# Head projections of a latent attention layer: key tiles first, values in 512 column blocks, exponentials in groups of three

## The chip, the cores and the metric

One core of one Trainium2 chip runs the whole program. Its engines are TensorE (PE; weight loads are shown as PEld), VectorE (DVE), ScalarE (ACT), GpSimd (POOL) and SyncE (SP), which issues the weight transfers. The metric is the device time of one execution in microseconds (us). The times of the kernel before are 4355.25, 4356.09 and 4361.63 us, median 4356.09.

## What is computed

The program is a first block of two layers, then a second block of two layers, an even one and an odd one. The change touches the odd one alone, and in it what stands between the latents and the attention:

```python
cq, ckv, kr = split(h @ w_in, (384, 640))              # 512 latents of x, 256 of the context (768 for keys and values)
q  = (rms_norm(cq, qa_norm) @ w_uq).reshape(n, 16, 64 + 32)
kv = (rms_norm(ckv, kva_norm) @ w_ukv).reshape(n, 16, 64 + 64)
q_nope = rms_norm(q[..., :64], qn_nope);  q_rope = rope_2d(rms_norm(q[..., 64:], qn_rope))
k_nope = rms_norm(kv[..., :64], kn_nope); v = kv[..., 64:]
k_rope = rope_2d(rms_norm(kr[:, :, None, :], kn_rope)) # one for all heads
# rms_norm(x, g) = x * rsqrt(mean(x * x) + eps) * g
y = softmax([q_nope, q_rope] @ [k_nope, k_rope] * scale) @ v @ w_out
```

## The kernel before

Each product in high precision is three TensorE products (`mm3`, L193 to L198): both factors are split into a high and a low part, and high with high, high with low and low with high are summed in PSUM. Weights come in tiles of 128 x 1024 floats (512 KB) through the `Stream` (L121): SyncE loads three slots ahead, `split_hi` on ScalarE (L167) copies the high part, `split_lo` on VectorE (L174) takes the low part as the rest. There are two slots of split tiles, so tile n+2 can be split once tile n is used (`used`). SyncE loads again after `lo_done`.

The odd layer (L1765) has 16 heads and works in two halves of 8 heads. In each half `HeadTiles` (L790) makes queries Q, keys K and values V, then `Attention` (L521) runs 32 units on them. Attention of a half begins on TensorE (L588) when all of the half's heads are out (`all_out`), and heads of the second half begin on TensorE when the first attention is done. So the stages stand one behind the other.

`HeadTiles` runs over a list of items. The first half begins with the rotary key `kr_tile` (8 x 3 products of 512 and 8 x 3 of 256 columns on the layer's input). Then for each pair of heads, four pairs a half: two `q_tile` items (9 products of 512 columns each), one `k_tile` (6 of 512 and 6 of 256), one `v_tile`: 36 products of 128 columns, with the latents as stationary and 128 weight columns as moving factor. A pair has two weight tiles of its own, each partly filled: 16 tiles for both halves. For each item but a value item:

- TensorE projects into two PSUM banks, chosen by the item's number; ScalarE squares them (L855) and copies them raw (L859).
- TensorE sums the squares over the rows of a head with a matrix of ones (L827, plain fp32) into banks 4 and 5.
- ScalarE takes the logarithm (`Ln`, L866) and then exp(-0.5 x) of it (`Exp`, L873) at once: the inverse root. The compiler puts an ACT_TABLE_LOAD before each of the two, and the profile shows it under the same line.
- VectorE multiplies raw, gain and inverse root: for queries and kr into a temporary (L890), for keys straight into K (L895).
- For queries and kr, TensorE turns the result with the rotation matrix (L835), VectorE multiplies it by the cosine (L905) and the sine (L907) and adds (L912); for kr the sum goes to eight heads of K, each add followed by a copy (L914).

TensorE's program takes, for item i: project i, sum the squares of i-1, turn i-2. ScalarE: square and copy i, then Ln and Exp of i-1. The raw copy and the temporary have two buffers, the root and its inverse one each. A value item is one ScalarE copy of 768 columns into V (L851). `split_hi` stands before the square.

Of the kernel before, what the change touches and what calls it, by code (L numbers as in the profile page):

```python
# [27 lines left out]
KC = D // 128  # L28
# [21 lines left out]
ODD_TILES = 6 + 2 * ODD_PAIRS + 8  # L50
# [3 lines left out]
def program(nc, io):  # L54
# [11 lines left out]
    with top:  # L66
# [858 lines left out]

        def setup():
# [838 lines left out]
        def odd_layer(CX):  # L1765
# [3 lines left out]
            with ExitStack() as ctx:  # L1769
                Hh, Hl = sb(ctx, "h_hi", [128, KC, T], F32R), sb(ctx, "h_lo", [128, KC, T], F32R)  # L1770
                Ch, Cl = sb(ctx, "c_hi", [128, KC, CT], F32R), sb(ctx, "c_lo", [128, KC, CT], F32R)
# [14 lines left out]
                def carve(at, shape):  # L1786
# [45 lines left out]
                def q_tile(n, h):  # L1832
                    def go(pe, i, done):
                        st.ready(pe, n)
                        for k in range(3):
                            m = mm3(pe, ps[:, 2 * (i % 2), :], st.at(n, 256 * k + 128 * h, 256 * k + 128 * h + 128),
                                    (Qh[:, k, :], Ql[:, k, :]), k == 0, k == 2)
                        m.then_inc(done, 1)
                    return go

                def k_tile(n):
                    def go(pe, i, done):
                        st.ready(pe, n)
                        for s, (a, e) in enumerate(((0, T), (T, N2))):
                            for k in range(2):
                                m = mm3(pe, ps[:, 2 * (i % 2) + s, 0:e - a], st.at(n, 256 * k, 256 * k + 128),
                                        (Lh[:, k, a:e], Ll[:, k, a:e]), k == 0, k == 1)
# [3 lines left out]
                def v_tile(n):  # L1851
# [11 lines left out]
                for half in range(2):  # L1863
                    items = []
                    if half == 0:
# [308 lines left out]
```

## Time and profile before

| what | us |
|---|---|
| median of three runs | 4356.09 |
| the profiled execution, its own time | 4354.72 |
| its span | 4353.2 |
| TensorE busy | 3941.1 (91%) |
| VectorE busy | 2270.2 (52%) |
| ScalarE busy | 1586.7 (36%) |

The span is what the profile shows from first to last instruction; the time has 1.5 us more around it. The page's groups of instructions name a line, an engine, what is written from what, their count, their busy time, the mean of one, and the idle time before them with what ended it. Averages over the span mix all layers. The odd layer's heads and attentions take 330 us of it, about 7.6%, and have to be read from windows of their own. The granted clock is a share of TensorE's full 2.4 GHz: 0.5 is its lower level, 1.2 GHz.

### The profile page before, as it was taken

What the parts mean: (1) busy time and instruction counts of PE and PEld (TensorE: products, weight loads), DVE (VectorE), ACT (ScalarE), POOL (GpSimd) and SP (SyncE); (2) the same over time, 40 slices, a digit from 0 to 9 for tenths busy, and PEclk for the clock granted to TensorE, in tenths of its full rate; (3) what the DMA queues carried; (4) which work ended last, traced back from release to release, by engine and by line L of the source; (5) the groups of instructions that cost most, each with busy time, mean ns of one, the idle gap of its engine ahead of it and who ended that gap; (6) DMA issues with size and microseconds to landing.
All of it is one profiled execution on the core that took longest, in us unless ns stands there. A gap on an engine that the chain in (4) does not pass through costs nothing. (4 is left out here: it accounts for less than half of the span.)

```text
span 4353.2 us, 52924 instructions
## 1 busy us (share of the span) xinstructions
PE 3941.1 (91%) x19258; PEld 3213.4 (74%) x19258; DVE 2270.2 (52%) x4044; ACT 1586.7 (36%) x2672; POOL 126.5 (3%) x188
## 2 busy tenths in 40 slices
PE   5999978999899997999969999699998679798999
PEld 3887766888688776688848887588887457576887
DVE  3665563666566666366632454355555344444555
ACT  2223353222322336322255454322221574743222
POOL 1000000000100000000000000000000000000000
PEclk9999989999999998999989999899999889899999
DMA  6443202443544220244211110121221110102332
GB/s 239 135 136 100 63 25 78 136 130 111 186 131 140 82 73 15 87 136 144 88 57 53 44 42 24 48 63 59 62 63 49 30 39 1 39 1 73 97 96 77
DMA packets 99854, 354.04 MB, mean 81 GB/s; under 512 B 11139, under 2 KB 14723, under 8 KB 98776
## 3 DMA queue, kind: packets, MB, share of 16 engines
q1 hardware_dynamic: 76632, 274.64, 20.8%
q0 software_dynamic: 18304, 70.33, 5.0%
q10 hardware_dynamic: 4736, 6.62, 0.4%
q8 instruction: 117, 1.92, 0.2%
q14 instruction: 65, 0.53, 0.0%
HBM read 345.73 MB, written 11.06 MB: 82 GB/s over the span
## 5 line engine op out<-in xcount | busy, mean ns | idle before, releaser
L167 ACT ACTIVATE w_hi<-w_raw 128x1024 fp32r<-128x1024 f32 x500 | 529.4, 1060 | 1902.5 <-PE ps L198 1733.9
L174 DVE TENSOR_TENSOR w_lo<-w_raw,w_hi 128x1024 fp32r<-128x1024 f32 x500 | 615.0, 1231 | 1161.2 <-ACT w_hi L167 1160.8
L196 PE MATMUL ps<-h_hi,w_hi 128*128 128x512 f32 (+1 forms) x2824 | 1094.2, 387 | 66.6 <-DVE h_lo L255 34.2
L197 PE MATMUL ps<-h_lo,w_hi 128*128 128x512 f32 (+1 forms) x2824 | 1083.3, 384 | 0.0
L198 PE MATMUL ps<-h_hi,w_lo 128*128 128x512 f32 (+1 forms) x2824 | 1082.1, 383 | 0.0
L196 PEld LDWEIGHTS ps<-h_hi,w_hi 128*128 128x128 f32 x2824 | 537.2, 190 | 192.3 <-issue 54.9
L198 PEld LDWEIGHTS ps<-h_hi,w_lo 128*128 128x128 f32 x2824 | 537.8, 190 | 103.9
L197 PEld LDWEIGHTS ps<-h_lo,w_hi 128*128 128x128 f32 x2824 | 538.8, 191 | 100.4 <-issue 1.4
L196 PE MATMUL ps<-a_hi,w_hi 128*128 128x512 f32 x1472 | 549.0, 373 | 3.3 <-DVE ctx_x L454 3.3
L197 PE MATMUL ps<-a_lo,w_hi 128*128 128x512 f32 x1472 | 546.8, 371 | 0.0
L198 PE MATMUL ps<-a_hi,w_lo 128*128 128x512 f32 x1472 | 546.0, 371 | 0.0
L196 PEld LDWEIGHTS ps<-a_hi,w_hi 128*128 128x128 f32 x1472 | 277.0, 188 | 57.2 <-DVE ctx_x L454 6.3
L198 PEld LDWEIGHTS ps<-a_hi,w_lo 128*128 128x128 f32 x1472 | 276.8, 188 | 49.1
L197 PEld LDWEIGHTS ps<-a_lo,w_hi 128*128 128x128 f32 x1472 | 277.1, 188 | 47.6
L454 DVE SCALAR_TENSOR_TENSOR x<-ps,x 128x512 f32<-128x512 f32 x352 | 231.5, 685 | 54.6 <-PE ps L198 52.6
L454 DVE SCALAR_TENSOR_TENSOR x<-ps,mod,x 128x512 f32<-128x512 f32 x256 | 188.0, 748 | 94.0 <-PE ps L198 94.0
L402 ACT ACTIVATE a_hi<-val 128x512 fp32r<-128x512 f32 (+1 forms) x184 | 106.0, 592 | 307.2 <-DVE val L438 307.2
L662 ACT ACTIVATE arena<-arena,nm 128x768 f32<-128x768 f32 (+3 forms) x160 | 130.9, 818 | 218.0 <-DVE nm L720 217.4
L240 PE MATMUL ps<-scratch,ones 128*128 128x512 f32 (+1 forms) x144 | 76.2, 682 | 98.8 <-ACT scratch L220 98.8
L612 PE MATMUL ps<-ident,arena 128*128 128x128 f32 x784 | 119.2, 284 | 31.7 <-DVE h_lo L775 26.4
L419 DVE TENSOR_TENSOR a_lo<-val,a_hi 128x512 fp32r<-128x512 f32 (+1 forms) x184 | 115.2, 640 | 62.5 <-ACT a_hi L402 62.5
L240 PEld LDWEIGHTS ps<-scratch,ones 128*128 128x128 f32 x144 | 27.3, 223 | 144.8 <-ACT scratch L220 124.2
(243 smaller groups left out, 4661.9 us busy)
## 6 DMA issues: line engine op xcount, KB each, us to landing
w_raw<-in_w_first SPq DMA_DIRECT2D x316, 512.0 KB, 3.6
w_raw<-in_w_mlp SPq DMA_DIRECT2D x128, 512.0 KB, 3.6
shared<-in_w_ada POOLq DMA_DIRECT2D x96, 512.0 KB, 4.3
w_raw<-in_w_odd SPq DMA_DIRECT2D x30, 512.0 KB, 3.6
w_raw<-in_w_even SPq DMA_DIRECT2D x26, 512.0 KB, 3.6
near_stage<-near_bias POOLq DMA_DIRECT2D x32, 256.0 KB, 2.9
bias_rows<-bias_line SPq DMA_DIRECT2D x1, 5120.0 KB
shared<-silu_cond POOLq DMA_DIRECT2D x4, 1024.0 KB, 4.9
```

The source lines that it names most:

```text
L167: act.activation(self.hi[:, n % H, :], self.raw[:, n % R, :], ACT.Copy).then_inc(self.hi_done, 1)
L174: dve.tensor_tensor(self.lo[:, n % self.n_hl, :], self.raw[:, n % self.n_raw, :], self.hi[:, n % self.n_hl, :].bitcast(F32), ALU.subtract) ...
L196: pe.matmul(out, lhs[0], rhs[0], start=start, stop=False)
L197: pe.matmul(out, lhs[0], rhs[1], start=False, stop=False)
L198: return pe.matmul(out, lhs[1], rhs[0], start=False, stop=stop)
L240: pe.matmul(self.acc(), ones[:, :], self.tmp["sq"][:, c % 2, 0:self.n], start=(c == 0), stop=(c == self.nk - 1)).then_inc(self.sum_done, 1)
L402: m = act.activation(self.hi[s][:, 2 * (c % 2) + j, :], self.val[s][:, j, :], ACT.Copy)
L419: m = dve.tensor_tensor(self.lo[s][:, a, :], self.val[s][:, j, :], self.hi[s][:, a, :].bitcast(F32), ALU.subtract)
L454: m = dve.scalar_tensor_tensor(out=stream["x"][:, o, :], in0=ps[:, self.down_bank(8 * c + o, s), 0:stream["n"]], scalar=self.gains(s, o), ...
L612: m = pe.transpose(ps[:, 4 + t % 2, 128 * j:128 * j + 128], tmp["s"][:, u % 2, 128 * (b + j):128 * (b + j) + 128], ident[:, :])
L662: act.activation(tmp["s"][:, u % 2, 0:n], tmp["s"][:, u % 2, 0:n], ACT.Exp, bias=tmp["nm"][:, u % 16:u % 16 + 1], scale=-1.0, accum_out=tm ...
```

## The change

Both halves now have five full weight tiles: one with the keys of all eight heads, three with the queries, one with the values. That makes 24 tiles in the layer's stream in place of 30. `HeadGroups` takes the place of `HeadTiles` in the odd layer (the even layer keeps the old class):

- Items: kr (first half only), four key items, eight query items. That is 13 items in the first half and 12 in the second. Values are no items: they are six blocks of 128 latents x 512 weight columns (6 products each), projected behind the last item, two before the last item's sums and four behind. Each is copied to V with one ScalarE copy of 512 columns.
- Exponentials: items are taken in groups of three. Ln of each item comes as before, one item behind the square; Exp of a whole group comes right behind the Ln of its last item. So roots have six buffers, raw copies five. Exp writes over the root, the scaling writes over the raw copy.
- VectorE: once a group's Exp are there, it scales all items of the group, then turns those that have a rotary part. On TensorE, item k's rotation stands g[-1] + 2 + (k - g[0]) iterations into the program, for a group g: two to four items behind where it stood.
- The fifth raw buffer: from item 5 on, the raw copy waits until the item five back is out (`item_out`).
- `split_hi` now stands behind the raw copy.
- The raw copies lie where the context's split input lay, the squares where the raw copies lay.

The core of the diff (indentation shortened):

```diff
-ODD_TILES = 6 + 2 * ODD_PAIRS + 8
+ODD_TILES = 6 + 2 * 5 + 8
...
+class HeadGroups:
+    RAW, ROOT = 5, 6
+    BLOCKS = 6
...
+        self.groups = [range(a, min(a + group, L)) for a in range(0, L, group)]
+        self.ends = {g[-1]: g for g in self.groups}
+        self.parts = [sum(not x["frees"] for x in items[:k]) for k in range(L + 1)]
+        self.ropes = [sum(x["rope"] for x in items[:k]) for k in range(L + 1)]
+        self.turn_after, at = {}, 0
+        for g in self.groups:
+            for k in g:
+                if items[k]["rope"]:
+                    at = max(at, g[-1] + 2 + k - g[0])
+                    self.turn_after.setdefault(at, []).append(k)
...
+    def value_bank(self, j):
+        return (2 * (len(self.items) % 2) + j) % 4
+    def tensor(self, pe):
+        items, w, L = self.items, self.w, len(self.items)
+        def sums(k):
+            pe.wait_ge(self.sq_done, k + 1)
+            if k:
+                pe.wait_ge(self.root_done, k)
+            for a, b in self.halves(items[k]["n"]):
+                m = pe.matmul(ps[:, 4 + a // 512, 0:b - a], items[k]["ones"], w["sq"][k % 2][:, a:b],
+                              start=True, stop=True)
+            m.then_inc(self.sum_done, 1)
+        def turn(k):
+            r = self.ropes[k]
+            pe.wait_ge(self.t_done, k + 1)
+            if r >= 2:
+                pe.wait_ge(self.sin_done, r - 1)
+            pe.matmul(ps[:, 6 + r % 2, 0:512], self.rot, w["raw"][k % self.RAW][:, 0:512],
+                      start=True, stop=True).then_inc(self.rotated, 1)
+        def value_block(j):
+            if j in (0, 2):
+                pe.wait_ge(self.raw_done, L - 1 + j // 2)
+            if j >= 4:
+                pe.wait_ge(self.v_out, j - 3)
+            return self.values["project"](pe, j, self.value_bank(j))
+        for i in range(max(L + 1, max(self.turn_after, default=0) + 1)):
+            if i < L:
+                if i >= 2:
+                    pe.wait_ge(self.raw_done, i - 1)
+                items[i]["project"](pe, i, self.st.used if items[i]["frees"] else self.projected)
+            if 1 <= i <= L:
+                if i == L:
+                    value_block(0).then_inc(self.v_mm, 1)
+                    value_block(1).then_inc(self.v_mm, 1)
+                sums(i - 1)
+                if i == L:
+                    for j in range(2, self.BLOCKS):
+                        value_block(j).then_inc(self.v_mm if j < self.BLOCKS - 1 else self.st.used, 1)
+            for k in self.turn_after.get(i, ()):
+                turn(k)
+    def scalar(self, act):
+        items, w, L = self.items, self.w, len(self.items)
+        def inverse_root(k):
+            act.wait_ge(self.root_done, k + 1)
+            root = w["root"][k % self.ROOT][:, 0:items[k]["n"]]
+            act.activation(root, root, ACT.Exp, scale=-0.5).then_inc(self.inv_done, 1)
+        for i in range(L + 1):
+            if i < L:
+                it = items[i]
+                if it["frees"]:
+                    act.wait_ge(self.st.used, it["frees"][-1] + 1)
+                else:
+                    act.wait_ge(self.projected, self.parts[i] + 1)
+                if i >= 2:
+                    act.wait_ge(self.sum_done, i - 1)
+                act.activation(w["sq"][i % 2][:, 0:it["n"]], self.pair(i, 0, it["n"]), ACT.Square
+                               ).then_inc(self.sq_done, 1)
+                if i >= self.RAW:
+                    self.item_out(act, i - self.RAW)
+                act.activation(w["raw"][i % self.RAW][:, 0:it["n"]], self.pair(i, 0, it["n"]), ACT.Copy
+                               ).then_inc(self.raw_done, 1)
+                for n in it["tiles"]:
+                    self.st.split_hi(act, n + self.st.n_hl)
+            if i >= 1:
+                k, n = i - 1, items[i - 1]["n"]
+                act.wait_ge(self.sum_done, k + 1)
+                if k >= self.ROOT:
+                    act.wait_ge(self.t_done, k - self.ROOT + 1)
+                act.activation(w["root"][k % self.ROOT][:, 0:n],
+                               ps[:, 4:6, :].rearrange("p a n -> p (a n)")[:, 0:n], ACT.Ln,
+                               bias=eps[:, 0:1], scale=items[k]["scale"]).then_inc(self.root_done, 1)
+                for e in self.ends.get(k, ()):
+                    inverse_root(e)
+        for j in range(self.BLOCKS):
+            if j < self.BLOCKS - 1:
+                act.wait_ge(self.v_mm, j + 1)
+            else:
+                act.wait_ge(self.st.used, self.values["tile"] + 1)
+            act.activation(self.values["dst"](j), ps[:, self.value_bank(j), :], ACT.Copy).then_inc(self.v_out, 1)
+        self.st.split_hi(act, self.values["tile"] + self.st.n_hl)
+    def vector(self, dve):
+        items, w, L = self.items, self.w, len(self.items)
+        def scale(k):
+            it, n = items[k], items[k]["n"]
+            raw, inv = w["raw"][k % self.RAW], w["root"][k % self.ROOT]
+            dve.wait_ge(self.inv_done, k + 1)
+            if it["rope"]:
+                dve.scalar_tensor_tensor(out=raw[:, 0:n], in0=raw[:, 0:n], scalar=it["gain"], in1=inv[:, 0:n],
+                                         op0=ALU.mult, op1=ALU.mult).then_inc(self.t_done, 1)
+                return
+            for r, dst in it["dst"]:
+                m = dve.scalar_tensor_tensor(out=dst(0, n), in0=raw[r, 0:n], scalar=it["gain"][r, :],
+                                             in1=inv[r, 0:n], op0=ALU.mult, op1=ALU.mult)
+            m.then_inc(self.t_done, 1)
+        def turn(k):
+            it, r, raw = items[k], self.ropes[k], w["raw"][k % self.RAW]
+            if it["rope"]:
+                if r:
+                    dve.wait_ge(self.out_done, r)
+                dve.wait_ge(self.t_done, k + 1)
+                dve.tensor_tensor(w["cos"], raw[:, 0:512], self.cos, ALU.mult).then_inc(self.cos_done, 1)
+                dve.wait_ge(self.rotated, r + 1)
+                dve.tensor_tensor(w["sin"], ps[:, 6 + r % 2, 0:512], self.sin, ALU.mult).then_inc(self.sin_done, 1)
+                dve.wait_ge(self.cos_done, r + 1)
+                dve.wait_ge(self.sin_done, r + 1)
+                for rows, dst in it["dst"]:
+                    m = dve.tensor_tensor(dst(0, 512), w["cos"][rows, :], w["sin"][rows, :], ALU.add)
+                    if it["n"] > 512:
+                        m = dve.tensor_copy(dst(512, it["n"]), raw[rows, 512:it["n"]])
+                m.then_inc(self.out_done, 1)
+        for i in range(L):
+            for n in items[i]["tiles"]:
+                self.st.split_lo(dve, n + self.st.n_hl)
+            for g in self.groups:
+                if g[-1] + 1 == i:
+                    for k in g:
+                        scale(k)
+                    for k in g:
+                        turn(k)
+        for k in self.groups[-1]:
+            scale(k)
+        for k in self.groups[-1]:
+            turn(k)
+        self.st.split_lo(dve, self.values["tile"] + self.st.n_hl)
+    def all_out(self, eng):
+        eng.wait_ge(self.v_out, self.BLOCKS)
+        eng.wait_ge(self.t_done, len(self.items))
+        eng.wait_ge(self.out_done, self.ropes[-1])
+    def item_out(self, eng, k):
+        if self.items[k]["rope"]:
+            eng.wait_ge(self.out_done, self.ropes[k] + 1)
+        else:
+            eng.wait_ge(self.t_done, k + 1)
...
-        Ch, Cl = sb(ctx, "c_hi", [128, KC, CT], F32R), sb(ctx, "c_lo", [128, KC, CT], F32R)
+        with ExitStack() as early:
+            Ch, Cl = sb(early, "c_hi", [128, KC, CT], F32R), sb(early, "c_lo", [128, KC, CT], F32R)
+        raw_slots = sb(ctx, "head_raw", [128, 2 * KC * CT])
...
-        w = {"raw": cx[:, 0:2 * N2].rearrange("p (a n) -> p a n", a=2), "sin": cx[:, 2 * N2:2 * N2 + 512],
-             "sq": carve(0, [2, N2]), "root": carve(2 * N2, [N2]), "inv": carve(3 * N2, [N2]),
-             "t": carve(4 * N2, [2, N2]), "cos": carve(6 * N2, [512])}
+        w = {"raw": [raw_slots[:, N2 * k:N2 * k + N2] for k in range(5)],
+             "root": [carve(N2 * k, [N2]) for k in range(6)],
+             "sq": [cx[:, N2 * k:N2 * k + N2] for k in range(2)],
+             "cos": carve(6 * N2, [512]), "sin": cx[:, 2 * N2:2 * N2 + 512]}
...
-                for j in range(6):
-                    t = slice(128 * j, 128 * j + 128)
-                    for k in range(2):
-                        m = mm3(pe, ps[:, 2 * (i % 2) + j // 4, 128 * (j % 4):128 * (j % 4) + 128],
-                                (Lh[:, k, t], Ll[:, k, t]), st.at(n, 256 * k + 128, 256 * k + 256), k == 0, k == 1)
...
+        def q_tile(n, h):
             def go(pe, i, done):
-                for j in range(6):
-                    t = slice(128 * j, 128 * j + 128)
-                    for k in range(2):
-                        m = mm3(pe, ps[:, 2 * (i % 2) + j // 4, 128 * (j % 4):128 * (j % 4) + 128],
-                                (Lh[:, k, t], Ll[:, k, t]), st.at(n, 256 * k + 128, 256 * k + 256), k == 0, k == 1)
+                for k in range(3):
+                    tile, c = n + (3 * h + k) // 8, 128 * ((3 * h + k) % 8)
+                    st.ready(pe, tile)
+                    m = mm3(pe, ps[:, 2 * (i % 2), :], st.at(tile, c, c + 128), (Qh[:, k, :], Ql[:, k, :]),
+                            k == 0, k == 2)
+                    if c == 896 and k < 2:
+                        m.then_inc(st.used, 1)
                 m.then_inc(done, 1)
+            return go
+        def v_block(n):
+            def go(pe, j, bank):
+                st.ready(pe, n)
+                t = slice(128 * j, 128 * j + 128)
+                for k in range(2):
+                    m = mm3(pe, ps[:, bank, :], (Lh[:, k, t], Ll[:, k, t]), st.at(n, 512 * k, 512 * k + 512),
+                            k == 0, k == 1)
+                return m
             return go
...
+            for h in range(8):
+                ends = {2: first + 1, 5: first + 2, 7: first + 3}
+                items.append({"project": q_tile(first + 1, h), "n": T, "ones": mla_ones[:, :],
+                              "scale": 1.0, "gain": gq[:, 0:1], "rope": True,
+                              "tiles": [ends[h]] if h in ends else [], "frees": [first + 3] if h == 7 else [],
+                              "dst": [(slice(0, 96), lambda a, b, c=h: Q[0:96, c, a:b])]})
+            values = {"project": v_block(first + 4), "tile": first + 4, "dst": lambda j: V[:, j, :]}
+            heads.append(HeadGroups(S, w, st, items, 3, values, rot[:, :], cos[:, :], sin[:, :]))
...
+    for half in range(2):
+h = slice(8 * half, 8 * half + 8)
+keys = ukv[:, :, h, 0].reshape(2, 128, 4, 128).transpose(1, 2, 0, 3).reshape(1, 128, 1024)
+queries = uq[:, :, h].transpose(1, 2, 0, 3).reshape(128, 3, 1024).transpose(1, 0, 2)
+values = ukv[:, :, h, 1].transpose(1, 0, 2, 3).reshape(1, 128, 1024)
+odd += [keys, queries, values]
```

## Rows read from the trace of the kernel before

**Rows 1.** Windows view: stretch, length, busy us (count) by engine, granted clock, DMA.

```profile
3463.42:3578.31 114.89, 90.71 (x366) 66.72 (x367) 48.95 (x68) 80.26 (x91) 0.00 (x0) 0.83 0.14 42
3578.31:3700.87 122.56, 111.92 (x721) 91.19 (x721) 58.12 (x184) 51.55 (x112) 0.00 (x0) 0.96 0.00 1
3700.87:3793.66 92.79, 72.20 (x313) 52.55 (x313) 38.97 (x48) 73.28 (x84) 0.00 (x0) 0.87 0.16 46
```

**Rows 2.** Groups of ScalarE, 3463 to 3794 us: busy, mean ns | idle.

```profile
L866 ACT ACT_TABLE_LOAD x25 | 32.1, 1283 | 0.4
L873 ACT ACT_TABLE_LOAD x25 | 32.1, 1283 | 0.4
...
L866 ACT ACTIVATE arena<-ps,eps 128x512 f32<-128x512 f32 (+1 forms) x25 | 19.1, 764 | 0.3
L689 ACT ACTIVATE arena<-ps 128x512 f32<-128x512 f32 x32 | 18.5, 578 | 6.9 <-PE ps L612 6.9
L167 ACT ACTIVATE w_hi<-w_raw 128x1024 fp32r<-128x1024 f32 x17 | 18.0, 1057 | 37.1 <-PE ps L198 37.1
L873 ACT ACTIVATE arena<-arena 128x512 f32<-128x512 f32 (+1 forms) x25 | 17.7, 707 | 0.3
L859 ACT ACTIVATE ctx_x<-ps 128x512 f32<-128x512 f32 (+1 forms) x25 | 16.8, 670 | 1.0
...
L851 ACT ACTIVATE v<-ps 128x768 f32<-128x768 f32 x8 | 6.3, 792 | 0.0
```

**Rows 3.** Timeline, a query tile's chain: start, length, instruction, idle before.

```profile
3508.30 1.28 ACT L866 ACT_TABLE_LOAD   x1
...
3509.59 0.69 ACT L866 ACTIVATE arena<-ps,eps 128x512 f32<-128x512 f32 x1
...
3510.43 1.10 PE L827 MATMUL ps<-arena,mla_ones 128*128 128x512 f32 x2 [1.32 <-ACT arena L866]
3511.59 0.63 ACT L873 ACTIVATE arena<-arena 128x512 f32<-128x512 f32 x1
...
3512.26 0.75 DVE L890 SCALAR_TENSOR_TENSOR arena<-ctx_x,q_gain,arena 128x512 f32<-128x512 f32 x1 [3.69 <-ACT arena L873]
```

**Rows 4.** Timeline of TensorE: neighbouring products, 128 and 512 columns.

```profile
3492.75 0.28 PE L198 MATMUL ps<-w_hi,ckv_lo 128*128 128x128 f32 x1
...
3492.86 0.28 PE L196 MATMUL ps<-w_hi,ckv_hi 128*128 128x128 f32 x1
...
3529.55 0.39 PE L196 MATMUL ps<-cq_hi,w_hi 128*128 128x512 f32 x1
...
3529.78 0.39 PE L197 MATMUL ps<-cq_lo,w_hi 128*128 128x512 f32 x1
```

**Rows 5.** The windows view, four stretches of 5 us, columns as in rows 1.

```profile
3465.00:3470.00 5.00, 5.00 (x15) 3.90 (x14) 0.00 (x0) 0.00 (x0) 0.00 (x0) 0.58 0.00 0
3490.00:3495.00 5.00, 4.36 (x34) 3.91 (x34) 4.90 (x12) 4.02 (x5) 0.00 (x0) 1.00 0.00 0
3515.00:3520.00 5.00, 5.00 (x25) 5.00 (x25) 2.07 (x4) 2.75 (x4) 0.00 (x0) 0.50 0.00 0
3700.00:3705.00 5.00, 4.13 (x11) 3.30 (x12) 0.77 (x4) 0.33 (x1) 0.00 (x0) 0.66 0.00 0
```

**Rows 6.** The timeline, the end of the second heads stretch.

```profile
3782.93 1.50 PE L827 MATMUL ps<-arena,head_ones 128*128 128x512 f32 x4
...
3784.27 1.02 PE L835 MATMUL ps<-arena,rot 128*128 128x512 f32 x2
...
3793.66 1.19 PE L588 MATMUL ps<-k,q 128*128 128x512 f32 x1 [8.36 <-DVE q L912]
```

**Rows 7.** The groups of VectorE over 3463 to 3794 us.

```profile
L890 DVE SCALAR_TENSOR_TENSOR arena<-ctx_x,q_gain,arena 128x512 f32<-128x512 f32 x16 | 12.0, 752 | 56.7 <-ACT arena L873 56.6
...
L907 DVE TENSOR_TENSOR ctx_x<-ps,sin 128x512 f32<-128x512 f32 x17 | 11.6, 684 | 0.0
...
L912 DVE TENSOR_TENSOR k<-arena,ctx_x 32x512 f32<-32x512 f32 x8 | 5.4, 677 | 0.1
```

More of the change, by code:

```diff
@@ L923, in all_out, with __init__, pair, halves @@
                     eng.wait_ge(self.out_done, self.ropes[-1])
+        class HeadGroups:
+            RAW, ROOT = 5, 6
+            BLOCKS = 6
+            def __init__(self, S, work, st, items, group, values, rot, cos, sin):
+                self.items, self.st, self.w, self.values = items, st, work, values
+                self.rot, self.cos, self.sin = rot, cos, sin
+                self.projected, self.sq_done, self.raw_done, self.sum_done = S("proj"), S("hsq"), S("raw"), S("hsum")
+                self.root_done, self.inv_done, self.t_done = S("hroot"), S("hinv"), S("ht")
+                self.rotated, self.cos_done, self.sin_done, self.out_done = S("rot"), S("cos"), S("sin"), S("hout")
+                self.v_mm, self.v_out = S("v_mm"), S("v_out")
+                L = len(items)
+                self.groups = [range(a, min(a + group, L)) for a in range(0, L, group)]
[8 more added lines that the diff above has]
+                            self.turn_after.setdefault(at, []).append(k)
+            def pair(self, i, a, b):
+                return ps[:, 2 * (i % 2):2 * (i % 2) + 2, :].rearrange("p a n -> p (a n)")[:, a:b]
+            @staticmethod
+            def halves(n):
+                return [(0, min(n, 512))] + ([(512, n)] if n > 512 else [])
+            def value_bank(self, j):
[131 more added lines that the diff above has]
+                    eng.wait_ge(self.t_done, k + 1)
@@ L1830, in kr_tile, with k_tile @@
                     project_x(pe, 5, 2 * (i % 2), xs).then_inc(done, 1)
[L1832 to L1841, printed above, removed]
+                def k_tile(n, p):
                     def go(pe, i, done):
@@ L1864, in odd_layer @@
                     items = []
+                    first = 6 + 5 * half
                     if half == 0:
-                        items.append({"project": kr_tile, "n": N2, "plain": False, "ones": mla_ones[:, :], "scale": 1.0,
-                                      "gain": vec("kr_norm", 1), "rope": True, "tiles": [5],
+                        items.append({"project": kr_tile, "n": N2, "ones": mla_ones[:, :], "scale": 1.0,
+                                      "gain": vec("kr_norm", 1), "rope": True, "tiles": [5], "frees": [5],
@@ L1868, in odd_layer @@
                                       "dst": [(kr_rows, lambda a, b, h=h: K[64:96, h, a:b]) for h in range(8)]})
                     for p in range(4):
-                        n = 6 + 2 * (4 * half + p)
-                        for h in range(2):
-                            items.append({"project": q_tile(n, h), "n": T, "plain": False, "ones": mla_ones[:, :],
-                                          "scale": 1.0, "gain": gq[:, 0:1], "rope": True, "tiles": [] if h == 0 else [n],
-                                          "dst": [(slice(0, 96), lambda a, b, c=2 * p + h: Q[0:96, c, a:b])]})
@@ L1875, in odd_layer @@
-                        items.append({"project": k_tile(n + 1), "n": N2, "plain": False, "ones": head_ones[:, :],
-                                      "scale": 1.0 / HD, "gain": vec("kn_norm", 1), "rope": False, "tiles": [],
+                        items.append({"project": k_tile(first, p), "n": N2, "ones": head_ones[:, :],
+                                      "scale": 1.0 / HD, "gain": vec("kn_norm", 1), "rope": False,
+                                      "tiles": [first] if p == 3 else [], "frees": [first] if p == 3 else [],
@@ L1884, in odd_layer @@
-                    heads.append(HeadTiles(S, w, st, items, rot[:, :], cos[:, :], sin[:, :]))
+                    for h in range(8):
[4 more added lines that the diff above has]
+                                      "dst": [(slice(0, 96), lambda a, b, c=h: Q[0:96, c, a:b])]})
```

15 lines of the change are left out of this document (3 added, 12 removed).

## The prediction

> **What bounds the kernel now.** I read the page's share of busy time first, and it misleads here: TensorE at 91% is a mean over all layers, and the change touches only the odd layer's heads. So I cut windows at the places where one stage hands over to the next: the first product of the rotary key, the first product of each attention, and the first product of the second half's heads [rows 1]. The reader is to see two head stretches, of 114.89 and 92.79 us (207.68 together), in which ScalarE is busy 80.26 and 73.28 us (70% and 79%), TensorE 90.71 and 72.20 us with a granted clock of 0.83 and 0.87, and VectorE under half. The attention between them has a clock of 0.96 and isn't touched. Since attention begins only when the last head is out, whatever a head stretch loses or gains counts fully.
>
> Next come ScalarE's groups over the same time [rows 2]. Of its 153.5 us in the two head stretches, 64.2 us are table loads: 25 under the logarithm's line and 25 under the exponential's, 1.283 us each, one ahead of every such instruction. The chain of one query tile shows what they do [rows 3]: load 1.28, logarithm 0.69, load 1.28, exponential 0.63, and only then does VectorE go on, after 3.69 us idle; TensorE stood 1.32 us for the logarithm. With a single root buffer and two of everything else, nobody gets ahead of this chain. So the stretch is bound by ScalarE's list, and TensorE waits in pieces of 1 to 3 us.
>
> The third view is TensorE's pace. Neighbours of 128 columns stand 0.11 us apart and neighbours of 512 columns 0.23 us [rows 4]: four times the columns for twice the time. The clock comes last [rows 5]: of the two windows full of a value item's 128 column products one shows 1.00 and one 0.50 for the whole 5 us. In the second TensorE had stood with gaps before, fell to its 1.2 GHz level, and stayed there as long as the 128 column products ran; three of the eight value items look like this. The windows at the start of each half show 0.58 and 0.66.
>
> **A yardstick.** To put a price on a rearranged order I wrote the three engines' lists out in program order and gave each instruction the duration of its row; each starts when its engine is free and the event it waits for is there, with 0.05 us for a hand-over (an exponential ends at 3512.22, VectorE starts at 3512.26) and 0.2 us for TensorE after a real wait (the logarithm ends at 3510.28, the sums begin at 3510.43) [rows 3]. The sums of squares take TensorE 0.86 us for 512 columns and 1.3 for 768 (3782.93 to 3784.27 [rows 6]), which is also the source of 0.86 for a rotation. Run on the order of before, at the full clock, this gives 96.6 and 81.7 us. The mean clocks 0.83 and 0.87 say that 34% and 26% of the stretches, 39 and 24 us, were at the lower level. Some 3 us of each lie in the idle end, and half of the rest is lost: 18 and 10.5 us. Together 114.6 and 92.2, against 114.89 and 92.79. The method carries.
>
> **What the change does, part by part.**
>
> *Table loads.* Groups of three give one load ahead of the group's logarithms and one ahead of its exponentials: 5 groups in the first half, 4 in the second, so 18 loads in place of 50. 32 x 1.283 = 41.1 us leave ScalarE [rows 2]. The trace shows the next instruction 1.29 us after a load starts and nothing besides, so 1.28 is the whole price. The Trainium skill (ScalarE: Activation LUTs, What ACT_TABLE_LOAD costs) puts a switch at about 2.66 us, a drain included; by that the 32 would be 85 us, but no row here has the drain. The same page (Table sets: the hidden batching unit) says that logarithm and exponential can share a set, by which there would be no load to save; the 25 and 25 loads of rows 2 say that this program doesn't use it.
>
> *Values.* 8 x 36 products at 0.11 us are 32 us at the full clock; 2 x 36 products at 0.23 us are 16.4 us [rows 4]. 15 us leave TensorE, and more at the lower level. ScalarE copies 12 x 0.58 us in place of 8 x 0.79 [rows 2], a wash.
>
> *Weight tiles.* Six fewer: 6.3 us off ScalarE [rows 2], 7.4 off VectorE, six transfers off SyncE's queue, which was waiting for slots and not for data. Worth nothing by itself beyond ScalarE's list.
>
> *New waits.* By list sums TensorE would have 62.4 and 51.9 us, ScalarE 53 and 47, VectorE 43 and 33. The bound moves to TensorE and to what makes it wait. At each group's edge ScalarE does load, three exponentials, square, copy, load and logarithm, about 6.5 us, while TensorE has two projections (4.1) and then waits for the root: 2.5 to 3.3 us once per group. In the first half, item 5's raw copy waits for the rotary key's output, whose eight adds (0.68 [rows 7]) and eight copies keep VectorE 6.5 us: ScalarE stands 6.3 us, with squares and logarithms queued behind that copy, and TensorE 4.8. Later a query tile's low part is queued behind item 5's turn on VectorE: TensorE stands 2.3 us. Each `q_tile` now checks its weight tile before each third: 16 more checks a half that nearly always find the tile there. [...]
>
> *The tail.* It gets longer. Before, the second half ended with 9.4 us from TensorE's last rotation to attention's first product, 8.36 of them idle [rows 6]. Now value blocks 4 and 5 wait for banks, that is for ScalarE's copies, which stand behind the last exponentials; the rotation of item 8 stands behind block 5; and on VectorE its sine and add, a 1.2 us low part, three scalings (0.75) and three turns (0.69 + 0.68 + 0.69 each [rows 7]) stand behind that rotation. From the last exponential that is 15.2 us.
>
> **The new order written out, at the full clock.** Second half: third key's exponential at 18.5 us, then the three query groups at 30.6, 43.2 and 55.3 (12.3 us each: 8.7 of products and sums, up to 2.6 of rotations, the edge's wait), end at 70.5. First half: 8.3 us for the rotary key, first group out at 24.1, then 41.9 (17.8: the stand for the rotary key's output), 53.6, 68.8 (15.2: three rotations and the late tile), 74.0 for the single last item, end at 87.4.
>
> **The sum.** Lower level at the start, as now [rows 5]: 2.9 and 1.7 us. Further stretches at the lower level cannot be read from before; between none and the 15 and 9 us of before I take two short ones a half, 3.4 us lost in each half, since gaps stay but no 128 column products prolong them. Hand-overs a little longer than 0.05: 1 us a half, since doubling them adds 1.4 and 0.7 to the new order. First half 87.4 + 2.9 + 3.4 + 1.0 = 94.7; second 70.5 + 1.7 + 3.4 + 1.0 = 76.6; with 1 us for the checks 172.3. Saved: 207.7 - 172.3 = 35.4 us. The profiled execution had a time of 4354.72, so 4319.3; the median of the runs is 1.4 us above it: 4320.7 us. Nothing ahead of the heads changes but where buffers lie; attention starts, as before, after an idle TensorE; the output projection's first two tiles are split ahead of attention, as before.
>
> **Rivals.** *The queues couple more tightly than my order says*, so that every group costs what the dearest ordinary one does, 15.2 us in place of about 12. For it: raw copy, rotation and low part wait across three queues. Against: the yardstick hit both halves of before within 0.6 us. Six groups x 3 us = 18 us less saved: 4338.
>
> *TensorE never waits inside a half.* Lists of 62.4 and 51.9 plus tails of 13 and 15 and the 4.6 at the start are 147 us: 61 us saved, 4295. Against: the key output's stand is in the program, whatever the durations.
>
> *The other side: the clock.* Gaps of 2 to 5 us at every group edge drop TensorE to 1.2 GHz, and it stays there. With all of both halves at that level my order gives 128.4 and 104.8 = 233.2 us, 25.5 more than now: 4381.6. Between that and 157.9 without any, it turns slower when TensorE is at the lower level for two thirds of the stretch. For it: before had 34% and 26%. Against: the long low stretches were those of the 128 column products, which are gone; 512 column products brought 1.00 back within the kernel's own first tile.
>
> *The change doesn't do what it says*: the compiler puts loads ahead of every exponential all the same. Nothing between three neighbouring exponentials asks for another table; I give it next to nothing, inside the first rival.
>
> **How the numbers follow.** My order 0.72 (its own range 4309 to 4331), tighter coupling 0.16, no waits 0.06, the clock 0.03, none of them 0.03. Range for 8 in 10: 4306 to 4338. A measurement of this kernel can tell 0.2%, 8.7 us, from no change; for that 26.7 of the 35.4 us would have to be lost, which only the far end of the coupling case or a middling case of the clock does: faster 0.94, same 0.04, slower 0.02.
>
> **What the profile after would show.** 18 loads; no 128 column products in the heads; ScalarE about 53 and 47 us busy in the stretches, TensorE at a clock of 0.85 to 0.95; the stretches 92 to 98 and 74 to 80 us long; a 6 us stand of ScalarE at a raw copy early in the first half; the tails 13 to 15 us from the last exponential. The prediction is wrong if the stretches are right but attention or later layers move by more than 3 us, if the clock is below 0.75, or if VectorE's turns stand in the way of more than one raw copy.

## The result and the profile after

Five executions of the changed kernel took 4322.10, 4330.21, 4331.93, 4334.69 and 4335.02 us, median 4331.93, against 4356.09 before: ratio 0.9942, 95% interval 0.993 to 0.9955, so 24 us or 0.6% faster. In a second group of runs the same kernel had a median of 4326.08 (ratio 0.9927, 0.9907 to 0.9947). The forecast was 4320.7, range 4306 to 4338.

The profiled execution is the fastest of the five, 4322.10 us with a span of 4320.5. Its windows, cut at the same events as [rows 1] (first heads, first attention, second heads; the columns are those of [rows 1]):

```profile
3462.05:3556.92 94.87, 74.89 (x258) 50.30 (x259) 44.46 (x65) 55.03 (x74) 0.00 (x0) 0.88 0.09 28
3556.92:3684.93 128.01, 117.32 (x720) 94.93 (x721) 59.10 (x185) 51.67 (x112) 0.00 (x0) 0.91 0.02 5
3684.93:3761.93 77.00, 60.84 (x204) 39.68 (x205) 34.49 (x45) 48.39 (x67) 0.00 (x0) 0.90 0.09 28
```

The heads take 94.87 and 77.00 us in place of 114.89 and 92.79, 35.8 us less, with ScalarE down from 80.26 and 73.28 us busy to 55.03 and 48.39. But the first attention, whose code is the same, takes 128.01 us in place of 122.56, at a clock of 0.91 in place of 0.96.

ScalarE's groups from 3462.05 to 3761.93 us, both head stretches and the attention between them (columns of [rows 2]; L1034 is the logarithm, L1010 the exponential, L1025 the raw copy, L1021 the square):

```profile
L1034 ACT ACTIVATE arena<-ps,eps 128x512 f32<-128x512 f32 (+1 forms) x25 | 19.1, 765 | 10.1 <-PE ps L969 10.0
L1025 ACT ACTIVATE head_raw<-ps 128x512 f32<-128x512 f32 (+1 forms) x25 | 16.8, 671 | 6.5 <-DVE k L1077 6.5
L1021 ACT ACTIVATE ctx_x<-ps 128x512 f32<-128x512 f32 (+1 forms) x25 | 16.7, 667 | 30.8 <-PE ps L198 30.8
...
L1034 ACT ACT_TABLE_LOAD x9 | 11.5, 1283 | 0.2
L1010 ACT ACT_TABLE_LOAD x9 | 11.5, 1283 | 0.2
```

50 loads have become 18. Where the logarithm used to wait for nothing (0.3 us before, the groups of [rows 2]: ScalarE was always late), it now waits 10.0 us for TensorE's sums, the square 30.8 us for projections, and the raw copy 6.5 us for VectorE. ScalarE's list no longer sets the length of the stretch.

The timeline of the first half at the stand behind the rotary key, and of the second half's end (columns of [rows 3]; L978 is the rotation, L1071 the sine, L1055 a scaling):

```profile
3500.39 0.60 ACT L1025 ACTIVATE head_raw<-ps 128x512 f32<-128x512 f32 x1 [6.55 <-DVE k L1077]
```

```profile
3744.48 1.67 ACT L1010 ACTIVATE arena<-arena 128x512 f32<-128x512 f32 x3
3746.06 2.04 ACT L1044 ACTIVATE v<-ps 128x512 f32<-128x512 f32 x4
...
3749.56 1.02 PE L978 MATMUL ps<-head_raw,rot 128*128 128x512 f32 x2
...
3750.61 0.69 DVE L1071 TENSOR_TENSOR ctx_x<-ps,sin 128x512 f32<-128x512 f32 x1 [9.20 <-PE ps L978]
...
3752.02 1.22 DVE L174 TENSOR_TENSOR w_lo<-w_raw,w_hi 128x1024 fp32r<-128x1024 f32 x1
3753.16 2.07 DVE L1055 SCALAR_TENSOR_TENSOR head_raw<-head_raw,q_gain,arena 128x512 f32<-128x512 f32 x3
...
3761.93 1.19 PE L588 MATMUL ps<-k,q 128*128 128x512 f32 x1 [3.60 <-DVE q L1075]
```

Here stand three of the places where the gain is given back. ScalarE stands 6.55 us at a raw copy until the rotary key is out. The last exponential ends at 3746.15 and attention starts at 3761.93, a tail of 15.8 us. In it VectorE idles 9.20 us for one rotation that is queued on TensorE behind the value blocks, which wait for ScalarE's value copies. Before, this tail was 4.35 us, because the last exponential belonged to a key item, which has no rotation:

```profile
3788.47 0.84 ACT L873 ACTIVATE arena<-arena 128x768 f32<-128x768 f32 x1
```

### The profile page after: what moved, and what is told of

Read it like the earlier page. It is cut to its first block and busy times, and to the rows that moved or that the text cites. A ratio compares the mean times of both kernels' runs of the same rounds, so it can differ in the third digit from the quotient of the medians.

```text
span 4320.5 us, 52368 instructions
## 1 busy us (share of the span) xinstructions
PE 3914.2 (91%) x19042; PEld 3185.2 (74%) x19042; DVE 2263.0 (52%) x4038; ACT 1536.5 (36%) x2638; POOL 125.4 (3%) x188
## 5 line engine op out<-in xcount | busy, mean ns | idle before, releaser
L198 PEld LDWEIGHTS ps<-a_hi,w_lo 128*128 128x128 f32 x1472 | 276.9, 188 | 48.8
```

The source lines that it names most:

```text
L198: return pe.matmul(out, lhs[1], rhs[0], start=False, stop=stop)
```

## Experiments

All times of head stretches are from one trace each; "heads" is the sum of both. The kernel before was traced three times, its heads are 207.7, 202.1 and 210.6 us (mean 206.8); the changed kernel twice, 171.9 and 171.7 (mean 171.8). Each variant has one trace, two_turn_early a second one (best_again). The old kernel's traces spread over 8.5 us, so a smaller difference that rests on single traces is weak evidence by itself.

**The same kernels again.** 

> The changed kernel once more, unaltered. Theory: the two head stretches repeat within 1 us (94.9 and 77.0), and what differs between executions is TensorE's granted clock in the other stages, so that the span follows the mean clock: 0.955 went with 4320.5, 0.951 with 4333. Rival: the head stretches themselves vary by several us.

> The kernel before, unaltered, for a second trace of it. Question: the forecast took 207.7 us for its two head stretches from one execution. Theory (what the clock does in the other stages made the median gain smaller than the forecast): the head stretches repeat within 2 us, and the part ahead of them lies anywhere between 3462 and 3473 us, as in the eight traces of kernels that don't differ there. Rival (the one execution was a slow one in the heads): 203 us or less.

> The same kernel, a third trace of it, with the same expectations as for the second.

The windows of both head stretches: the changed kernel's second trace, then the second and third trace of the kernel before.

```profile
3470.58:3564.78 94.20, 72.86 (x258) 48.62 (x259) 44.44 (x65) 55.03 (x74) 0.00 (x0) 0.90 0.09 28
3688.29:3765.75 77.46, 61.46 (x205) 40.26 (x205) 34.48 (x45) 48.37 (x67) 0.00 (x0) 0.90 0.09 28
```

```profile
3462.60:3571.91 109.31, 88.45 (x366) 65.01 (x367) 48.93 (x68) 79.83 (x91) 0.00 (x0) 0.84 0.15 44
3694.56:3787.32 92.76, 72.20 (x312) 52.62 (x313) 38.95 (x48) 73.28 (x84) 0.00 (x0) 0.87 0.16 46
```

```profile
3466.23:3581.18 114.95, 90.78 (x366) 66.73 (x367) 48.94 (x68) 80.30 (x91) 0.00 (x0) 0.83 0.14 42
3703.74:3799.34 95.60, 77.13 (x312) 56.12 (x313) 38.96 (x48) 73.31 (x84) 0.00 (x0) 0.82 0.15 45
```

The changed heads repeat within 0.7 us. The old ones spread over 8.5 us, where 2 were expected: before_once (4348.45 us in all) has 202.1, under the 203 that the rival named, and before_twice (4357.83 us) has 210.6. The forecast's base of 207.7 lies within 1 us of the mean of the three. So it was fair, but in part by luck: before_once would have moved the forecast saving by 5.6 us. What differs between executions is the rest: the first head stretch begins at 3462.05 in one trace of the changed kernel and at 3470.58 in the other, and nothing ahead of it differs. The run times follow the mean clock: of the changed kernel's nine executions the three at 0.951 took 4329.4 to 4335.0 us, the two at 0.955 and 0.956 took 4322.1 and 4319.3.

**Loads put back.**

```diff
-heads.append(HeadGroups(S, w, st, items, 3, values, ...))
+heads.append(HeadGroups(S, w, st, items, 1, values, ...))
```

> Group size 1 in place of 3: each exponential behind its own logarithm again, 50 loads in place of 18, all else of the change kept. Theory (the queues' order sets the stretch, and with five raw buffers most of a load lies beside TensorE's work): the hand schedule gives 87.8 and 75.8 us in place of 87.4 and 70.5 at the full clock, so the two head stretches together grow by 6 us, to about 178. Rival (the loads removed are what the change gained): 32 x 1.283 = 41 us, to about 213.

```profile
3462.50:3556.19 93.69, 73.41 (x258) 48.16 (x259) 45.51 (x65) 76.47 (x90) 0.00 (x0) 0.92 0.10 28
3682.00:3764.06 82.06, 60.68 (x204) 38.90 (x205) 35.37 (x45) 69.92 (x83) 0.00 (x0) 0.92 0.08 26
```

ScalarE is 43 us busier (76.47 and 69.92 against 55.03 and 48.39), all of it the 32 loads and what comes with them, and the heads take 175.8 us, 3.9 more; the first half is even shorter. The median was 4324.86, no different from the changed kernel's 4326.08 in the same runs. So the exponentials in groups of three, as this kernel makes them, are worth about 4 us in one trace and nothing that the total can show. The rival's 41 us falls. Read the other way: with all 50 loads in place the rest of the change already takes 31 of the 35 us off the old heads.

**Groups of two.** The same edit with 2.

> Group size 2 in place of 3: 26 loads in place of 18. Theory: shorter groups free TensorE and VectorE earlier and shorten the tail by one turn; the schedule gives 78.2 and 68.1 in place of 87.4 and 70.5, so 11.6 us less in the head stretches although 8 loads (10.3 us of ScalarE) come back. Rival (each load is paid): 10 us more.

```profile
3462.93:3546.37 83.44, 69.34 (x259) 47.27 (x259) 44.49 (x65) 60.49 (x78) 0.00 (x0) 0.93 0.11 32
3671.17:3743.44 72.27, 59.42 (x205) 39.08 (x205) 34.43 (x45) 53.62 (x71) 0.00 (x0) 0.90 0.10 30
```

Heads 155.7 us, 16 less than in threes, with 8 loads more; median 4306.68, ratio to before 0.9892 (0.9873 to 0.9911). The Trainium skill (ScalarE: Activation LUTs, Rules for kernel authors) says to group by table set and to do all of one set before switching. Here that holds only up to the point where the group makes others wait: from one to two it gains 20 us in the heads, from two to three it loses 16. Two of these waits can be read off. ScalarE's stand at the raw copy is 6.5 us in threes, and 0.0 in twos and in ones. The two tails, from the last exponential to attention, are 14.6 and 15.8 us in threes, 12.5 and 13.6 in twos, 9.5 and 10.1 in ones.

**Loads taken away, old order and new.** In the heads' traces table loads stand ahead of logarithms and exponentials only, none ahead of a copy.

```diff
-act.activation(..., ACT.Exp, scale=-0.5)      # the inverse roots of the odd layer's heads
+act.activation(..., ACT.Copy, scale=-0.5)
```

> The kernel before, with the odd layer's exponentials of the roots replaced by scaled copies, so that nothing switches the table between logarithms: some 48 of 50 loads fall away (heads get the wrong scale; that part of the computation is changed). Theory: in the old order, with two buffers, loads lie on the path. The hand schedule gives 81.3 and 68.0 us at the full clock in place of 96.6 and 81.7, 29 us less, and up to 10 more where the clock rises. Rival (loads lie beside TensorE's work in the old order too, as one_per_group showed for the new one): under 6 us less.

> The changed kernel with the same replacement: 16 of its 18 loads fall away (heads get the wrong scale). Theory: the schedule gives 81.4 and 62.9 in place of 87.4 and 70.5, 13.6 us less: the two loads at each group's edge are still on the path, although spreading them out (one_per_group) cost next to nothing. Rival (loads are all hidden now): under 3 us less.

The kernel before without loads, then the changed kernel without loads:

```profile
3465.75:3551.92 86.17, 76.24 (x366) 56.16 (x367) 48.95 (x68) 48.28 (x67) 0.00 (x0) 0.96 0.19 55
3677.47:3748.84 71.37, 63.35 (x312) 46.98 (x313) 39.15 (x48) 44.43 (x62) 0.00 (x0) 0.96 0.21 60
```

```profile
3471.76:3559.51 87.75, 69.51 (x259) 47.36 (x259) 44.45 (x65) 44.30 (x66) 0.00 (x0) 0.91 0.09 30
3683.06:3749.24 66.18, 58.12 (x204) 38.29 (x205) 34.30 (x45) 40.05 (x61) 0.00 (x0) 0.94 0.11 32
```

Four loads are left in the two stretches of either kernel, in each half one ahead of the first logarithm and one ahead of attention's first exponential, which found its table loaded before. So 46 loads fall away from the old order and 14 from the new one, and not 48 and 16 as the expectations had it.

In the old order the loads were worth 49 us: heads 157.5 in place of 206.8 for 46 loads, 59 us of ScalarE. The medians say the same: 4307.23 in place of 4355.63, 48.4 us. 29 were expected from the order at the full clock and up to 10 from the clock, which rose from 0.83 and 0.87 to 0.96 although the 128 column products were all still there; both terms were too small together by 10. In the changed kernel the last 14 are worth 18 us (153.9 in place of 171.8), as much as they take on ScalarE, 18.0 us (13.6 expected). Without loads old and new order differ by 3.6 us in one trace each, and not at all in the medians (4307.23 and 4308.96). So what the whole rewrite gains depends on the loads: it is a way to live with them. Once they are gone, fewer tiles and wide value products are offset by the new order's own waits.

**Narrow value products in the new order.**

```diff
-m = mm3(pe, ps[:, bank, :], latents, st.at(n, 512 * k, 512 * k + 512), ...)
+for c in range(0, 512, 128):      # four products of 128 columns for each of 512
+    m = mm3(pe, ps[:, bank, c:c + 128], latents, st.at(n, 512 * k + c, 512 * k + c + 128), ...)
```

> Each value block as four times 128 weight columns in place of one 512 column product (144 products a half in place of 36), all else kept. Theory: 24 x 0.11 = 2.7 us a block in place of 1.4; the schedule gives 94.6 and 76.6 in place of 87.4 and 70.5, 13 us more in the two head stretches, and up to 7 us more where the clock falls and stays low under these products. Rival (value products lie beside ScalarE's chain anyway): under 3 us more.

```profile
3464.39:3579.92 115.53, 94.88 (x367) 71.33 (x367) 44.44 (x65) 55.24 (x74) 0.00 (x0) 0.78 0.07 23
3703.38:3786.49 83.11, 68.70 (x312) 48.90 (x313) 34.46 (x45) 48.48 (x67) 0.00 (x0) 0.91 0.08 26
```

Heads 198.6 us, 26.8 more; median 4349.55 of ten executions, 23.5 us over the changed kernel's in the same runs, ratio to before 0.9988. In this order most of the gain is gone without the wide products. The second half grew by 6.1 us, as the schedule had it, with the same 128 column products at a clock of 1.00. The first grew by 20.7: TensorE had waited 2.80 us for the value tile's low part, began the blocks at 3537.42, fell to its lower level within 3 us and stayed there to their end. Six neighbouring windows of 5 us, 3540 to 3570, read 0.50 with TensorE busy all the time; the first of them:

```profile
3540.00:3545.00 5.00, 5.00 (x25) 5.00 (x25) 1.00 (x2) 0.00 (x0) 0.00 (x0) 0.50 0.37 129
```

**Two raw buffers and 50 loads.**

```diff
-RAW, ROOT = 5, 6
+RAW, ROOT = 2, 6          # and groups of one, as in one_per_group
```

> As one_per_group, but with two raw buffers in place of five. Theory (in the new order with 50 loads it is the raw buffers that keep ScalarE going past VectorE's turns): item i's raw copy now waits for the output of item i - 2; the schedule gives 121.9 and 100.8 us at the full clock in place of 87.8 and 75.8, 59 us more, to about 235 for both. Rival (the order of items and the value blocks carry it, buffers don't matter): under 10 us more.

```profile
3467.99:3599.98 131.99, 83.86 (x259) 52.93 (x259) 45.80 (x65) 77.55 (x90) 0.00 (x0) 0.84 0.07 20
3722.51:3832.05 109.54, 70.01 (x205) 42.66 (x205) 35.65 (x45) 70.90 (x83) 0.00 (x0) 0.86 0.07 20
```

```profile
PE ps L969 <- ACT arena L1034: 31.9, 12, 8.4
DVE head_raw L1055 <- ACT arena L1010: 31.0, 8, 4.6
ACT head_raw L1025 <- DVE q L1075: 22.0, 6, 4.0
```

Heads 241.5 us, 65.8 more than with five buffers (59 expected), and 4390 us for the single execution: slower than before. The waits of the first half (who waits for whom, us in total, times, longest) show the ring: ScalarE's raw copy waits for VectorE's output, VectorE for the exponential, TensorE for the logarithm. So the five buffers are what makes 50 loads harmless in one_per_group.

**A rotation moved ahead.** Groups of two, and in each half the rotation that stood behind the last value blocks:

```diff
 if i == L:
-    for j in range(2, self.BLOCKS): value_block(j)...
-for k in self.turn_after.get(i, ()): turn(k)
+    for j in (2, 3): value_block(j)...
+    for k in self.turn_after.get(i, ()): turn(k)
+    for j in (4, 5): value_block(j)...
+# for i != L the rotations stay where they were
```

> Groups of two, and the rotation that stood behind value blocks 4 and 5 moved ahead of them (behind block 3). Theory: VectorE's sine, add, low part, scalings and last turns start before ScalarE's value copies are through; the schedule gives 76.2 and 64.1 in place of 78.2 and 68.1 of two_per_group, 6 us less in the head stretches, about 4301 us. Rival (the tail is set by the value copies): within 2 us of two_per_group.

> two_turn_early once more, with more rounds. Theory: head stretches of 148 us in both, 24 us under the changed kernel, 59 under the kernel before; the median between 4296 and 4309 us. Rival (its gain over two_per_group in the stretches is not kept): median at or above 4307.

```profile
3471.19:3552.13 80.94, 69.20 (x258) 47.29 (x259) 44.53 (x65) 60.43 (x78) 0.00 (x0) 0.94 0.12 33
3677.06:3744.45 67.39, 57.74 (x205) 38.50 (x205) 34.40 (x45) 53.66 (x71) 0.00 (x0) 0.95 0.10 32
```

Heads 148.3 us in both traces (80.87 and 67.40 in the second), 7.4 less than two_per_group. The medians were 4306.23 and 4297.19 us, 49 and 57 us under the kernel before in the same runs, ratios 0.9878 (0.9858 to 0.9899) and 0.9868 (0.9851 to 0.9884). It is the best version by its heads and by the second group of runs. The first median doesn't tell it from two_per_group's 4306.68, and no runs had both side by side; in its first trace the heads began at 3471 us, in two_per_group's at 3463.

**Idle ends filled.** As two_turn_early, with three fp32 products that nobody reads behind the last value block and three behind the last rotation of each half.

> As two_turn_early, with TensorE's idle time at each half's end filled by products that nobody reads: three plain fp32 products of 512 columns behind value block 5 and three behind the last rotation. Theory of the clock: the lower level at attention's start follows the idle end of the heads; filled, attention starts at 1.00 and each attention is 2 us shorter. Against it, the fill itself can delay the last rotations by up to 1.7 us at the full clock and 4 at the lower one. Rival: no attention stretch changes, heads are 1 to 4 us longer.

Windows about the first attention's start (3552.13 without the filling, 3556.45 with it): without it, then with it.

```profile
3552.00:3557.00 5.00, 4.87 (x8) 2.52 (x8) 2.32 (x5) 0.67 (x1) 0.00 (x0) 0.50 0.27 105
```

```profile
3555.00:3560.00 5.00, 4.19 (x12) 1.90 (x10) 3.62 (x9) 0.80 (x1) 0.00 (x0) 1.00 0.32 105
```

Both attentions now start at the full clock (the second's first 5 us read 1.00 in place of 0.66), as the theory had it, but the heads are 4.6 us longer (83.63 and 69.33). The first attention took 120.90 us in place of 124.93, the shortest of all traces, the second 125.35 in place of 123.67: only one of the two became shorter. The median, 4304.57, doesn't differ from two_turn_early's 4306.23.

## Why the prediction was right, and where it wasn't

**The bound.** Right. ScalarE's chain with its loads held the old heads: taking only the loads away brought 49 us, more than the 35 of the whole change.

**The written-out order.** Right, and better than its error bars. 94.7 and 76.6 us were forecast, 94.9 and 77.0 came, and the second trace has 94.2 and 77.5. Its details came too: 18 loads, 55 and 48 us of ScalarE (53 and 47 forecast), clocks of 0.88 and 0.90, a stand of 6.55 us at item 5's raw copy (6.3), a second tail of 15.8 us from the last exponential (15.2). The same order gave the sign and rough size of every variant: 6 us for groups of one (3.9 came), 11.6 less for groups of two (16), 6 less for the rotation (7.4), 59 more for two buffers (66). It was too small where the clock went with it: 13 to 20 for narrow products (26.8), 29 to 39 for the old loads (49).

The order also came group by group. The exponentials of the first three groups of the second half:

```profile
3703.06 2.32 ACT L1010 ACTIVATE arena<-arena 128x768 f32<-128x768 f32 x3
...
3717.42 1.89 ACT L1010 ACTIVATE arena<-arena 128x768 f32<-128x768 f32 x3
...
3732.08 1.67 ACT L1010 ACTIVATE arena<-arena 128x512 f32<-128x512 f32 x3
```

From the stretch's start at 3684.93 the four groups end at 20.5, 34.4, 48.8 and 61.2 us. The order at the full clock had 18.5, 30.6, 43.2 and 55.3, before the 1.7 us for the start and the 4.4 for clock and hand-overs. That the sum then came within 0.5 us in each half is closer than its terms allow, and in part luck. By the yardstick's own rule clocks of 0.88 and 0.90 cost 9.9 and 6.2 us, and the sum had 6.3 and 5.1. Either the order at the full clock is some 5 us too long or the rule asks too much where TensorE waits more; no run separates the two. The 1 us for the checks is a term that no run shows: across the thirds of a query tile the products stand 0.23 us apart (3714.63 to 3716.00 us), as inside them.

**The attribution.** The part by part list led with 41.1 us of loads. That was the right count and says nothing of the gain: one_per_group puts them back for 3.9 us. The prediction had the reason in its own *new waits* and *tail*, but never set them against the loads. What three at a time saves on ScalarE it gives back at the rotary key's output and in the tails, as the three group sizes show. The group edges, which the prediction names too, weren't measured apart. The wide value products, listed at 15 us, were worth 26.8: 13.3 by the schedule and 13.5 through the clock in one half. These prices overlap and don't add up to 35: 49 for the loads in the old order, 26.8 for the wide products and 65.8 for the buffers in the new one. No run put five buffers or wide products alone into the old order, so how much each would bring there stays open.

**The total.** The measured median is 11 us above the forecast, inside the range. The step that failed is the last of the sum: "the median of the runs is 1.4 us above it", and attention as before. The heads lost 35.8 us against a forecast of 35.4; the profiled execution's time fell by 32.6 (4354.72 to 4322.10), the median by 24.2. The missing 3 us are the first attention, 5.45 us longer at a clock of 0.91, less 2.3 us by which the other stages were shorter. That attention moved by more than 3 us while the head stretches were right is one of the signs by which the prediction called itself wrong: it came, and the assumption behind it, that nothing outside the heads changes, doesn't hold for these traces. The other 8.4 are that the profiled execution lies 9.8 us under its median, and not 1.4. Three windows show where its clock fell in that attention:

```profile
3595.00:3600.00 5.00, 2.67 (x9) 2.00 (x9) 1.31 (x5) 1.95 (x7) 0.00 (x0) 0.67 0.00 0
3600.00:3605.00 5.00, 5.00 (x21) 4.38 (x20) 1.19 (x4) 1.20 (x3) 0.00 (x0) 0.50 0.00 0
3605.00:3610.00 5.00, 5.00 (x26) 3.49 (x25) 2.04 (x6) 1.72 (x4) 0.00 (x0) 0.81 0.01 3
```

Summed over the traces of each kernel (three of before, two of after; us):

| stage | before | after |
|---|---|---|
| up to the first heads | 3462.6 to 3466.2 | 3462.1, 3470.6 |
| both heads | 202.1 to 210.6 | 171.9, 171.7 |
| both attentions | 245.2 to 248.3 | 251.6, 251.5 |
| the rest | 433.9 to 434.3 | 435.0, 434.1 |

The means differ by 35.0 us in the heads and by 7 the other way in all other stages. That leaves 28 us, and all executions together show 27 (means of 4355.7 for 32 of before and 4328.5 for nine of after). Whether the changed heads make the attention's clock fall more often stays open. Both traces of after have one attention of 128.0 us, and none of the twelve traces of other kernels goes beyond 126; but it was the first attention in one trace and the second in the other, and values_128, with the same groups and tail order, has 123.5 and 124.9. In both the fall follows a stand of TensorE some 38 us into the attention. From the second trace: its second attention, a window behind the stand in it, and a window at the same stand in its first attention:

```profile
3765.75:3893.75 128.00, 117.37 (x721) 95.02 (x721) 59.09 (x185) 51.66 (x112) 0.00 (x0) 0.91 0.02 5
3810.00:3815.00 5.00, 5.00 (x21) 4.39 (x21) 1.62 (x5) 1.62 (x3) 0.00 (x0) 0.50 0.00 0
3600.00:3605.00 5.00, 2.89 (x20) 2.22 (x18) 2.37 (x10) 2.42 (x9) 0.00 (x0) 1.00 0.00 0
```

So the stand is there each time and the clock doesn't always fall at it. No run was made that could separate an effect of the change from chance.

**The rivals.** Tighter coupling (4338, by its own working 4338.7) and no waits at all (4295) didn't come. The total, 4331.93, lies between the forecast and the coupling rival, but the heads leave that rival nothing: they are 171.9 us, where it needs some 190. The clock rival had the wrong place: it named the heads and gave it all or nothing; what it took there is near what the sum had, and what moved was outside them. In values_128 it took 13.5 us of one half (20.7 us more where the full clock explains 7.2).

## What to carry to other kernels

A count of removed instructions is not a gain. Write the engines' lists out in order with measured durations, try the group size and buffer depth in that schedule, and only then choose: here two beat three by 16 us in the heads, and moving one rotation ahead of two value blocks brought 7. Before believing the last few us of a total, compare the unchanged stages of several traces: the part ahead of the heads moved by up to 11 us between executions here, so a change of 10 us is told by the windows of its own stage and not by a median of three.

## What the runs showed of the hardware that was not expected

- TensorE can be busy without a pause and stay at its lower level: 30 us at 0.50 in values_128 under 128 column products. Under the wide products at the same place the changed kernel's windows read 0.66 for the first 5 us and 1.00 for the next 10. The 128 column products alone don't do it: in the second half of values_128 the same blocks ran at 1.00, and the heads of before_no_loads have a mean clock of 0.96 with all of theirs. TensorE was busy 2.20 us of the 5 ahead of the first half's blocks (from 3537.42) and 4.59 of the 5 ahead of the second's (from 3756.89). That the stand ahead makes the difference fits these rows and wasn't tested by itself.
- Identical code ahead of the heads ended between 3462.05 and 3472.82 us in the fourteen traces. The mean clock up to there is 0.96 in the trace with 3462.05 and 0.95 in the one with 3472.82. Over 27 executions of the kernel before a straight line gives 2.2 us for 0.001 of mean clock, over the nine of the changed kernel 2.8.
- A table load costs what the queue around it makes of it: 1.283 us each time by the profile; in the length of the heads 1.1 us each in the old order (49 us for 46), 0.1 us each when 32 are put back into the new one with five buffers, 1.3 us each for the last 14 (18 us).
